# Weighing and releasing expert blocks in twos, with an eight-block ring, in a Hymba/PEER encoder step

## What is computed

```
u = expert_u[eidx]
a = einsum('thkd,td->thk', u, xb)
w = (g * gelu(a)).astype(xb.dtype)
out = einsum('thk,thkd->td', w, expert_v[eidx])
```

## Time and profile before

| | |
|---|---|
| median of 3 runs | 3794.66 us (3793.25 to 3795.22) |
| profiled execution | 3796.45 us, its span 3794.6 us |
| granted PE clock, mean | 0.783 of full speed |
| busy share: PE / DVE / ACT / POOL | 72% / 61% / 18% / 29% |
| gathers of experts, queue 0 | 1217.47 MB, 78.1% of 16 engines' span |
| other hardware queue, q1 | 57.42 MB, 4.2% |
| chain that ended last | PE 37%, DMA 35%, DVE 11%, issue 7%, ACT 6%, POOL 3% |

### The profile page before, as it was taken

One profiled execution on the slowest core, in us unless ns is written; L12 is line 12 of the kernel. 1 busy time (PEld: TensorE's weight loads), 2 busy tenths in 40 slices (PEclk: granted clock), 3 DMA queues, 4 the chain that ended last, 5 costly groups with the idle time before them and its releaser, 6 DMA issues.

```text
span 3794.6 us, 39042 instructions
## 1 busy us (share of the span) xinstructions
PE 2750.9 (72%) x13359; PEld 1028.7 (27%) x13359; DVE 2313.9 (61%) x6166; ACT 698.1 (18%) x2341; POOL 1091.4 (29%) x1179
## 2 busy tenths in 40 slices
PE   7999997767766766776667667666766766776665
PEld 4455544732212211221222122122212212221111
DVE  2333342747766775776677577667757766875544
ACT  2333332211112111111211111111111111111111
POOL 0000000023333333333333333333333333333332
PEclk9999998767867777776787788678778767776666
DMA  5000003259999999999999999999999999999998
GB/s 200 17 17 17 23 30 146 83 223 406 421 421 405 404 421 401 421 399 422 402 421 403 406 421 407 421 403 421 403 407 421 403 422 406 408 413 421 421 421 335
DMA packets 193446, 1277.37 MB, mean 337 GB/s; under 512 B 22624, under 2 KB 26336, under 8 KB 44384
## 3 DMA queue, kind: packets, MB, share of 16 engines
q0 software_dynamic: 167184, 1217.47, 78.1%
q1 hardware_dynamic: 26064, 57.42, 4.2%
HBM read 1255.40 MB, written 12.32 MB: 334 GB/s over the span
## 4 chain that ended last, share of the span: by engine, by line
PE 37%; DMA 35%; DVE 11%; issue 7%; ACT 6%; POOL 3%; SPq 1%; DVEq 0%; POOLq 0%; ACTq 0%
DMA arena<-in_experts,arena 34%; PE PS L1319 14%; PE PS L1136 7%; DVE arena L921 6%; PE PS L1346 5%; POOL arena L593 3%; ACT arena L801 3%; PE PS L1229 3%; PE PS L1305 2%; PE PS L1113 2%; PE PS L1218 1%; PE PS L1178 1%; ACT arena L795 1%; DVE arena L1000 1%; DVE arena L997 1%
## 5 line engine op out<-in xcount | busy, mean ns | idle before, releaser
L921 DVE CUSTOM_DVE_ANT_0 arena<-arena,PS 128x1024 f32<-128x1024 f32 x1152 | 1382.4, 1219 | 932.8 <-DMA arena<-in_experts,arena 486.7
L593 POOL DMA_INDIRECT arena<-in_experts,arena x1152 | 1082.8, 940 | 2031.4 <-PE PS L1319 1622.6
L1305 PE MATMUL PS<-arena 96*128 96x512 bf16 x2304 | 827.8, 460 | 825.4 <-DVE arena L921 778.5
L1319 PE MATMUL PS<-arena 128*32 128x512 f32 x4608 | 931.3, 952 | 111.2 <-ACT arena L801 60.2
L1305 PEld LDWEIGHTS PS<-arena 96*128 96x128 bf16 x2304 | 162.9, 104 | 1532.0 <-DVE arena L921 1278.9
L795 ACT ACTIVATE arena<-arena 128x4 f32<-128x4 f32 x288 | 59.2, 205 | 2047.3 <-DVE arena L921 2035.8
L1319 PEld LDWEIGHTS PS<-arena 128*32 128x32 f32 x4608 | 164.3, 150 | 683.9 <-issue 380.6
L1346 PEld LDWEIGHTS PS<-arena 128*128 128x128 f32 x2304 | 277.0, 200 | 86.4 <-issue 86.2
L1136 PE MATMUL PS<-arena 128*128 128x512 f32 (+1 forms) x720 | 287.6, 552 | 3.8 <-ACT arena L627 2.3
L1346 PE MATMUL PS<-arena 128*128 128x128 f32 x2304 | 290.0, 287 | 0.0
L801 ACT ACTIVATE arena<-arena 128x1 f32<-128x1 f32 x1152 | 244.8, 283 | 9.9 <-ACT arena L795 0.2
(11 more groups left out here) (129 smaller groups left out, 1579.3 us busy)
## 6 DMA issues: line engine op xcount, KB each, us to landing
arena<-in_experts,arena POOLq DMA_INDIRECT x1152
arena<-in_w_in SPq DMA_DIRECT2D x4, 2048.0 KB, 15.7
arena<-in_w_query POOLq DMA_DIRECT2D x8, 1024.0 KB, 16.9
arena<-arena SPq DMA_DIRECT2D x108, 64.0 KB
h_scratch<-arena SPq DMA_DIRECT2D x9, 512.0 KB, 2.6
arena<-h_scratch SPq DMA_DIRECT2D x9, 512.0 KB, 8.2
out<-arena SPq DMA_DIRECT2D x9, 512.0 KB
arena<-in_x_prompt SPq DMA_DIRECT2D x8, 512.0 KB, 3.5
```

The source lines that it names most:

```text
L593: pool.indirect_dma_start(out=uv[r], out_offset=None, in_=experts, in_offset=bass.IndirectOffsetOnAxis(ap=expert_T[t % 2][:, tok:tok + 1], ...
L921: dve.tensor_tensor_reduce(uv[r][:, 0:D], uv[r][:, 0:D], xb(n), 1.0, 0.0, ALU.mult, ALU.add, a_dot[(n // 4) % 2][:, n % 4:n % 4 + 1]).then ...
L1305: mm = pe.matmul(PS[:, 2 + 2 * (n % 2) + c, :], pick[0:96, j:j + 1].broadcast_to([96, P]), x3[t % 2][0:96, g, 512 * c:512 * c + 512], star ...
L1319: mm = pe.matmul(PS[32 * g:32 * g + 32, ACC + c, :], wz[n % 2][:, g, 31 - f:63 - f], uv[r][:, D + 512 * c:D + 512 * c + 512], start=(f == ...
```

## The change

The ring has eight buffers, the last eight of the former ten places, and block 0 starts in the third of them. So the first six blocks lie where they lay. Gelu, gated weights, weighing and release are done for two blocks at a time: `two_used` takes the place of `four_used`, and POOL waits before every second gather. PE weighs the first two blocks of a four between the second and the third spread, and the other two behind the fourth. In a two, the loop over the halves of `v` is outside and the loop over the two blocks inside. `collect` moves from behind the first dot of four 1 to behind the second dot of four 0.

```diff
-RING = 10
-FIRST_BLOCK = 4
+RING = 8
+FIRST_BLOCK = 2
-COLLECT_AT, SQUARES_AT, FINISH_AT = 1, 4, 5
+COLLECT_AT, SQUARES_AT, FINISH_AT = 0, 4, 5
...
-        uv = [arena_t[:, RING_AT + 2 * D * ((r + FIRST_BLOCK) % RING):][:, 0:2 * D] for r in range(RING)]
-        assert STATE_AT == RING_AT + 2 * D * RING
+        uv = [arena_t[:, STATE_AT - 2 * D * RING + 2 * D * ((r + FIRST_BLOCK) % RING):][:, 0:2 * D] for r in range(RING)]
+        assert STATE_AT >= RING_AT + 2 * D * RING
...
-                        if n >= RING and (n - RING) % 4 == 0:
-                            pool.wait_ge(four_used, (n - RING) // 4 + 1)
+                        if n >= RING and (n - RING) % 2 == 0:
+                            pool.wait_ge(two_used, (n - RING) // 2 + 1)
...
-                        act.wait_ge(dots_ready, 4 * n + 4)
-                        act.activation(a_gelu[n % 2], a_dot[n % 2], ACT.Gelu).then_inc(gelu_ready, 1)
-                        act.wait_ge(gelu_ready, n + 1)
-                        if n >= 2:
-                            act.wait_ge(four_used, n - 1)
-                        for g in range(4):
-                            tok = 32 * g + f
-                            act.activation(wz[n % 2][:, g, 31:32], a_gelu[n % 2][:, g:g + 1], ACT.Copy,
-                                           scale=gate_T[t % 2][:, tok:tok + 1]).then_inc(wgt_ready, 1)
+                        for q in range(2):
+                            pair = slice(2 * q, 2 * q + 2)
+                            act.wait_ge(dots_ready, 4 * n + 2 * q + 2)
+                            act.activation(a_gelu[n % 2][:, pair], a_dot[n % 2][:, pair], ACT.Gelu).then_inc(gelu_ready, 1)
+                            act.wait_ge(gelu_ready, 2 * n + q + 1)
+                            if n >= 2:
+                                act.wait_ge(two_used, 2 * n + q - 3)
+                            for g in range(2 * q, 2 * q + 2):
+                                tok = 32 * g + f
+                                act.activation(wz[n % 2][:, g, 31:32], a_gelu[n % 2][:, g:g + 1], ACT.Copy,
+                                               scale=gate_T[t % 2][:, tok:tok + 1]).then_inc(wgt_ready, 1)
...
-                        dve.wait_ge(gelu_ready, n // 4 - 1)
+                        dve.wait_ge(gelu_ready, 2 * (n // 4) - 2)
...
-                    dve.wait_ge(four_used, FOURS * (t + 1))
+                    dve.wait_ge(two_used, 2 * FOURS * (t + 1))
...
-                            if t and f == COLLECT_AT and i == 0:
+                            if t and f == COLLECT_AT and i == 1:
...
-                def weigh_experts(n, c):
+                def weigh_experts(n, q):
                     t, f = n // FOURS, n % FOURS
-                    if c == 0:
-                        pe.wait_ge(wgt_ready, 4 * n + 4)
+                    pe.wait_ge(wgt_ready, 4 * n + 2 * q + 2)
+                    if q == 0:
                         if f == 0 and t:
                             pe.wait_ge(acc_free, t)
                         if n == 0:
                             pe.wait_ge(h_ready, 4 * NT)
-                    for g in range(4):
-                        r = (4 * n + g) % RING
-                        mm = pe.matmul(PS[32 * g:32 * g + 32, ACC + c, :], wz[n % 2][:, g, 31 - f:63 - f],
-                                       uv[r][:, D + 512 * c:D + 512 * c + 512], start=(f == 0), stop=(f == FOURS - 1))
-                    if c == 1:
-                        mm.then_inc(four_used, 1)
+                    for c in range(2):
+                        for g in range(2 * q, 2 * q + 2):
+                            r = (4 * n + g) % RING
+                            mm = pe.matmul(PS[32 * g:32 * g + 32, ACC + c, :], wz[n % 2][:, g, 31 - f:63 - f],
+                                           uv[r][:, D + 512 * c:D + 512 * c + 512], start=(f == 0), stop=(f == FOURS - 1))
+                    mm.then_inc(two_used, 1)
...
                         spread_x(4 * n + 3)
+                        weigh_experts(n, 0)
                         spread_x(4 * n + 4)
                         spread_x(4 * n + 5)
-                        weigh_experts(n, 0)
                         weigh_experts(n, 1)
```

More of the change, by code:

```diff
@@ L422, in build @@
         wgt_ready = sem("wgt_ready")
-        four_used = sem("four_used")
+        two_used = sem("two_used")
         acc_free = sem("acc_free")
```

## The result

The changed kernel takes 3817.29 us (median of 5 runs, 3816.08 to 3818.50). The kernel before took 3795.22 us on the same chip (5 runs). The ratio is 1.0058, with a 95% interval of 1.0043 to 1.0073. So the change costs 22 us where 10 us less were forecast. The profiled execution of after took 3818.5 us, its span 3816.7 us, and the mean granted clock rose from 0.783 to 0.883.

The account below looks back on a forecast made before the run. DMA's gathers were taken to bound the kernel, with rests of 17.75 us nearly all there is to gain. Rests -14, start +4 and end -0.44 sum to -10.4 us: 3784 us, range 3775 to 3804.

Parts of the forecast that it names:

- ACT and waits ... nothing: On ACT, 288 more Gelus, 60 us, cost nothing, since it mostly waits for dots; POOL's doubled waits have only gathers behind.
- PE spreads two blocks and can weigh the first two at once, since their dots ran during `q`: On PE after `q`: first weighing, 1.92 us at the upper clock, hides in 3.1 us before the second can start.
- The rests of rows 2, -14: DMA's eight largest rests, 17.75 us together, mostly in fours with `q`, shrink: -14 us, bounds -17.75 and more than nothing.
- The clock behind it: PE's clock: upper level expected in most fours with `q`, as the new order puts a weighing into PE's wait.
- Width times (1.01 - share): Sizes DMA's rests from stretch width and DMA share: eight stretches, together 17.75 us, nearly all there is to gain.
- A two takes as long as a four: On PE, weighing two blocks takes as long as four did, 1.92 or 3.64 us by clock; bounds half and double.
- The start, +4: At the start POOL has issued eight blocks, not ten, so stock ends 5.0 us sooner: +4 us, bounds 0 and +4.6.
- `collect`, nothing: At a tile's start, `collect` behind the second dot is worth nothing, since no rest of DMA lies there.
- The drain between tilings: On PE, a drain at each tiling change could cost 6.4 us, leaving the sum 4 us better instead of 10.
- The slower one: Rival, 0.18: PE weighs behind `q` at the lower clock, 3.64 us, granted under about 0.6; rests deepen, 3828 us at least.
- No change: Rival, 0.34: rests move instead of going, the first two due 5.0 us earlier while DVE's selection holds dots; 3787 to 3802.

Follow-up runs that it names:

- run 1: Changed kernel with the last tile's squares moved on ACT from place 4 (a tile's fifth four) to place 6, finish from 5 to 7: 3796.01 us, 0.9999 of before.
- run 5: Changed kernel with ACT doing its routing steps and squares after the first two's Gelu and copies, squares still at place 4: 3794.70 us, 0.9996 of before.
- run 7: Changed kernel with the squares at place 9, behind another pair of `q`, and the finish at place 10: 3801.73 us, 1.0014 of before.
- run 8: Control: the kernel before the change, with its squares at place 6 and the finish at place 7: 3797.04 us, 1.0000 of before.
- run 4: Changed kernel with ten buffers instead of eight and the squares at place 6: 3791.72 us, 0.9988 of before.
- run 2: Changed kernel, still eight blocks in twos, with PE again making the next two spreads ahead of both weighings: 3968.83 us, 1.0454 of before.
- run 9: Changed kernel with ten blocks, still in twos, and the old PE order, next two spreads ahead of both weighings: 3794.45 us, 0.9993 of before.

## Why the prediction was wrong, point by point

**"ACT and waits ... nothing"** is the step that failed. It counted ACT's own new instructions and not what already stood ahead of the Gelu in ACT's list. Nor does the description of ACT's order ahead of the prediction name the squares. "PE spreads two blocks and can weigh the first two at once, since their dots ran during `q`" leans on the same gap: the dots were in, but ACT reached them last. At the other fours with `q` only the copy stands ahead, and the new order works there as foreseen. At place 4 the squares add two table loads of 1.28 us each, a root and a pass over the tile. The squares make the harm: in run 1 Gelu still comes 3.5 us behind the second dot (1854.71 + 1.22 to 1859.41), for the copy of `q` alone, and PE stands for 0.43 us instead of 4.49. Price: 38.2 us of rests, of which 21 us of time came back when the squares moved. Runs 1 and 5 take it away by two different edits, run 7 moves it, and run 8 shows that the squares cost nothing before.

The Trainium skill ("ScalarE: Activation LUTs", What ACT_TABLE_LOAD costs) gives about 1283 ns for a load, which these rows show, and another 1380 ns for a drain at each switch. The rows show no such drain: the load at 1199.84 follows the squares' last instruction, and the root begins 0.01 us after the load ends.

**The rests of rows 2, -14.** In the changed kernel they went entirely, -17.75, at the upper bound. But that was luck: it holds only beside the rest at place 4. In run 1, without it, the stretches from place 6 on lose 29.0 us by pace, as much as the 28.4 of before; with ten blocks (run 4) it is 20.4. So this term was mis-sized too: over all 260 windows run 1 loses 4.7 us less than before, where 14 were forecast. The clock behind it was right: 0.75 to 0.88 over the long stretch, and a weighing of 1.91 us behind `q` at the upper level. What failed is the step from a rest to a gain, "Width times (1.01 - share)". It assumes that DMA at a share near 1 runs at full pace, and that no new loss comes up elsewhere when a rest goes. Run 1 lost 19.7 us of rests and got 10.7 back as thin pace. Even without the slip at place 4 the change is worth nothing measurable with eight blocks (run 1), and at most some 4 us with ten (run 4).

**A two takes as long as a four.** Right: 1.91 and 3.63 us for eight instructions, beside 1.92 and 3.64 for sixteen. Run 2 fits the reason given, two strips idle: there two twos stand right behind each other, on four strips, and take 3.66 us together at a granted clock of 0.50 (3554 to 3558).

**The start, +4.** Right in place and nearly in size: 3.0 us.

**`collect`, nothing.** Right. The view of waits, which answers to the earlier trace rows:

```profile
PE PS L1322 <- DVE arena L1027: 4.2, 7, 0.6
```

**The drain between tilings.** In after the spread at 1207.07 begins just before the modelled end of the weighing, 1203.51 + 3.63 = 1207.14. As in the rows of before, nothing of it shows.

**The rivals.** The slower one didn't happen as told: its condition was a granted clock under about 0.6 behind `q`, and it was 0.93 to 1.00 in the four stretches above. The weighings of 3.63 us at place 4 stand behind the 4.49 us in which PE waits for ACT. In run 1, behind 0.43 us, the weighing at that place takes 1.91, so they aren't the cause. "No change" had the right door, the first two due 5 us earlier, but looked for DVE's selection behind it. Its words that rests move instead of going fit run 1, whose 3796.01 us lies in its range.

## What to carry to other kernels

When a wait is split so that half of the work is due earlier, read the in-order list of every engine on the way between the old due time and the new. What stood there without harm is on the path now. A smaller ring and a finer release are one trade: with the old order on PE eight blocks cost 173 us and ten nothing. And a rest of DMA that goes isn't all gain: read the pace in GB/s beside the busy share, over the whole stage and not only where the rest stood.

## What was not expected of the hardware

DMA's busy share and its pace come apart when little is queued. In the stretch without routing, two kernels that are alike but for the ring move 388 GB/s at a share of 0.98 with eight blocks and 421 GB/s at 1.01 with ten (runs 2 and 9), so 3% less share goes with 8% less pace. Only the size of the ring and the place where it begins differ between these two. The traces show where the missing part goes. In these 300 us run 2 has 16037 packets and run 9 has 17412; with 16 engines at these shares, a packet takes 0.293 us on average in run 2 and 0.278 in run 9. So the share counts longer packets as busy time. Why some packets take longer was not tried.
